# Router's last tile in halves and in another order, first up product behind one gathered chunk, state turns, bias columns and counts moved into experts 0 and 1

## What is computed

```python
logits = h.astype(F32) @ w_router.astype(F32) + b_router.astype(F32)
top_val, top_idx = lax.top_k(logits, TOP_K)          # 4 of 32
gates = jax.nn.softmax(top_val, axis=-1)
...
gu = xblk.astype(F32) @ w_gate_up[e].astype(F32) + b_gate_up[e].astype(F32)
gate, up = gu[:, :D_FF], gu[:, D_FF:]
gate = jnp.minimum(gate, SWIGLU_LIMIT)
up = jnp.clip(up, -SWIGLU_LIMIT, SWIGLU_LIMIT)
glu = gate * jax.nn.sigmoid(SWIGLU_ALPHA * gate)
return ((up + 1.0) * glu) @ w_down[e].astype(F32) + b_down[e].astype(F32)
```

## Time and profile before

| what | us |
|---|---|
| three runs | 1222.46, 1224.19, 1226.62 |
| median | 1224.19 |
| the profiled execution's own time | 1225.74 |
| its span (first to last instruction) | 1223.7 |
| TensorE busy | 1194.6 |
| VectorE busy | 456.5 |
| ScalarE busy | 259.2 |
| last load issued | 1175.5 |

### The profile page before, as it was taken

How to read it: one execution, slowest core, us unless ns; L and a number is a source line. 1 busy time by engine, 2 the same in 40 slices (tenths; PEclk the granted TensorE clock), 3 DMA queues, 4 the chain that set the end, 5 groups by cost and what they waited for, 6 DMA issues and landing times.

```text
span 1223.7 us, 18270 instructions
## 1 busy us (share of the span) xinstructions
PE 1194.6 (98%) x7828; PEld 576.3 (47%) x7828; DVE 456.5 (37%) x963; ACT 259.2 (21%) x633; POOL 45.7 (4%) x105
## 2 busy tenths in 40 slices
PE   8999999999999999999999999999999999999997
PEld 6776777745433444444443444444443434343332
DVE  3367777754322332333232232333331332222234
ACT  3114434522221211111120112111111111120113
POOL 8000110100000000000000000000000000000000
PEclk9999999999999999999999999999999999999999
DMA  9732202498999999999999999999999999999994
GB/s 286 178 104 70 79 3 73 143 397 324 418 429 428 426 427 428 427 432 423 432 430 428 431 432 431 427 431 429 434 432 428 430 429 431 433 431 428 428 422 160
DMA packets 46236, 436.11 MB, mean 356 GB/s; under 512 B 9269, under 2 KB 24696, under 8 KB 29386
## 3 DMA queue, kind: packets, MB, share of 16 engines
q1 hardware_dynamic: 44916, 431.35, 85.2%
q0 software_dynamic: 1152, 3.54, 0.9%
q10 hardware_dynamic: 86, 0.02, 0.0%
HBM read 430.01 MB, written 4.89 MB: 355 GB/s over the span
## 4 chain that ended last, share of the span: by engine, by line
PE 84%; DMA 14%; DVE 1%; ACT 0%; issue 0%; SPq 0%; DVEq 0%; ACTq 0%
PE bank L1555 30%; PE bank L1589 15%; DMA ring<-in_w_gate_up 11%; PE bank L865 10%; PE bank L1530 7%; PE bank L1619 4%; PE bank L1327 3%; PE bank L1580 2%; DMA ring<-in_w_down 2%; PE bank L1080 1%; PE bank L852 1%; PE bank L1610 1%; PE bank L894 1%; PE bank L1057 1%; DMA hx<-in_state_shift 0%; PE bank L1650 0%
## 5 line engine op out<-in xcount | busy, mean ns | idle before, releaser
L1555 PE MATMUL bank<-ring,mix 128*64 128x512 f32 x1504 | 343.9, 597 | 5.9 <-DMA ring<-in_w_gate_up 5.9
L1555 PEld LDWEIGHTS bank<-ring,mix 128*64 128x64 f32 x1504 | 101.5, 136 | 204.3 <-issue 198.0
L1589 PE MATMUL bank<-ring,mix 128*64 128x512 f32 x736 | 167.8, 597 | 2.1 <-DMA ring<-in_w_down 2.0
L2854 DVE TENSOR_TENSOR hTb<-bank,w2a 128x512 f32<-128x512 f32 x32 | 22.1, 692 | 371.0 <-PE bank L1580 371.0
L2121 ACT ACTIVATE mix<-bank,nf 128x256 f32<-128x256 f32 x64 | 26.9, 470 | 454.1 <-PE bank L1530 454.1
L865 PE MATMUL bank<-hTb,ring 128*128 128x328 f32 (+1 forms) x416 | 121.9, 443 | 0.8 <-DVE hTb L2323 0.4
L1555 PE MATMUL bank<-mix 128*64 128x512 f32 x496 | 111.4, 595 | 4.1 <-DMA mix<-in_w_gate_up 3.9
L2906 DVE TENSOR_TENSOR mix<-mix,bank 128x512 f32<-128x512 f32 x70 | 48.2, 689 | 160.0 <-PE bank L1619 160.0
L1589 PEld LDWEIGHTS bank<-ring,mix 128*64 128x64 f32 x736 | 49.9, 136 | 91.0 <-issue 87.6
L865 PEld LDWEIGHTS bank<-hTb,ring 128*128 128x128 f32 x416 | 76.4, 190 | 34.0 <-issue 2.2
L1555 PEld LDWEIGHTS bank<-mix 128*64 128x64 f32 x496 | 35.3, 137 | 73.9 <-issue 69.9
(11 more groups left out here) (442 smaller groups left out, 1145.7 us busy)
## 6 DMA issues: line engine op xcount, KB each, us to landing
ring<-in_w_gate_up SPq DMA_DIRECT2D x31, 4096.0 KB, 25.6
ring<-in_w_gate_up SPq DMA_DIRECT2D x32, 2048.0 KB, 16.3
ring<-in_w_down SPq DMA_DIRECT2D x16, 4096.0 KB, 28.1
mix<-in_w_gate_up SPq DMA_DIRECT2D x11, 4096.0 KB, 26.3
ring<-in_w_down SPq DMA_DIRECT2D x11, 2048.0 KB, 16.5
mix<-in_w_down SPq DMA_DIRECT2D x5, 4096.0 KB, 29.6
mix<-in_w_gate_up SPq DMA_DIRECT2D x9, 2048.0 KB, 15.0
ring<-in_w_in SPq DMA_DIRECT2D x14, 1024.0 KB, 5.6
```

Source lines behind the costliest of these rows:

```text
L1555: last_ = mm(b_[64 * half:64 * half + 64, :].rearrange("s (p q) -> s p q", q=4), toks, cols[:, half], start=(c == 0), stop=(c == KT - 1))
L1589: last_ = mm(b_[r:r + 64, :], lhs, w[:, o:o + NCOL], start=(j == 0 and q == 0), stop=(j == 1 and q == 3))
L2854: v.tensor_tensor(halves(gg), halves(banks[3][:, :]), bias(e, 0), ALU.add).then_inc(S("g1"), 1)
```

## The change

1. The last half tile of the router (tile 1, columns 512 to 1023) is added, turned and copied in two quarters (`turn_half`, `out_add(4)`), and the logits of that tile wait for the quarters at products 4 and 6, and not once at the start. The selection of tile 0 is made half before, half behind these steps. `fold(2)` goes ahead of the rank products, and the gathers of samples and tile 0 are spread anew around them.
2. Chunk 1 of the first gather is put into bank 2, so that chunks 0 and 1 are in separate banks. Chunk 0 is signalled, scaled and copied by itself; the first up product waits for it alone (`chunk_bias_ready` 1).
3. `gather_first(2)`, `counts`, `sample_states(0)`, `(1)` and `turn_bias` move behind up products of expert 0, `sample_states(2)` and `(3)` into expert 1. The unit `bias` goes; its turn raises `unit_filled` as the third one beyond the units (`BIAS`). ScalarE's and VectorE's parts follow, and ScalarE's exponentials for the gates stand between the second and third pair of chunks.
4. SyncE's load of the down bias moves from ahead of piece 7 to ahead of piece 10 and waits for `BIAS`.

```diff
-        STURN = [banks[1], banks[1], banks[6], banks[7]]
+        STURN = [banks[6], banks[7], banks[6], banks[7]]
+        BIAS = len(UNITS) + 3
...
-            sync.wait_ge(S("unit_filled"), U("bias", 1))
-            load(bdr, A["b_down"][0], "w00_bdr_in")
             sync.wait_ge(S("gathered"), 1)
             load_piece(7)
             for k in range(FIRST, len(PIECES)):
...
+                if k == FIRST + 1:
+                    sync.wait_ge(S("unit_filled"), BIAS)
+                    load(bdr, A["b_down"][0], "w00_bdr_in")
                 load_piece(k)
...
+            def turn_half(x):
+
+                pe.wait_ge(S("xo_ready"), 6 + x)
+                b_ = free("h2T", 4 + x)
+                for c_ in range(2):
+                    o_ = 512 + 256 * x + P * c_
+                    last_ = nc.tensor.transpose(b_[:, P * c_:P * c_ + P], h[:, 1, o_:o_ + P], ident[:, :])
+                filled(last_, "h2T")
...
+                    if n_ == 2 and c_ in (4, 6):
+                        pe.wait_ge(S("h2T_ready"), 3 + c_ // 2)
...
-            gather_samples(0, 6)
-            turn(4)
-            gather_samples(6, KT)
-            sample_states(0)
+            gather_samples(0, 2, 3, 4, 5)
+            turn_half(0)
+            turn_half(1)
             logits(2)
-            pe.wait_ge(S("sel_ready"), 2)
-            gather_rows(0, 1)
+            gather_samples(1, 6, 7)
+            fold(2)
             free("rank", 1)
             ranks_of_others(2)
-            fold(2)
-            gather_rows(1, KT)
+            pe.wait_ge(S("sel_ready"), 2)
+            gather_rows(0, 4)
             ranks(1)
-            sample_states(1)
-            turn_bias()
+            gather_rows(4, KT)
             pe.wait_ge(S("sel_ready"), 3)
             gather_first(0)
-            gather_first(2)
-            counts()
...
-                    if part == 0 and c % 2 == 0:
+                    if e + c == 0:
+                        pe.wait_ge(S("chunk_bias_ready"), 1)
+                    elif e == 0 and c == 1:
+                        pe.wait_ge(S("xg_ready"), 1)
+                    elif part == 0 and c % 2 == 0:
                         pe.wait_ge(S("xg_ready"), 4 * q + c // 2 + 1)
                     up(e, c)
-                    if e == 0 and c in (1, 3):
-                        gather_first(c + 3)
-                    if e == 0 and c in (4, 5):
-                        sample_states(c - 2)
+                    if e == 0 and c in (0, 1, 3):
+                        gather_first(c + 3 if c else 2)
+                    if e == 0 and c == 2:
+                        counts()
+                    if e == 0 and c > 5:
+                        sample_states(c - 6)
+                    if e == 0 and c == 7:
+                        turn_bias()
+                    if e == 1 and c in (2, 4):
+                        sample_states(1 + c // 2)
...
+            choose_exact(sel_0, TORD[1], 0, 2)
             out_add(4)
-            choose_exact(sel_0, TORD[1]).then_inc(S("sel_ready"), 1)
```

More of the change, by code:

```diff
@@ L232, in psum_units @@
     end("xo", 4)
-    add("h2T", 1, (2,))
+    add("h2T", 2, (2, 1))
     add("logit", 1, (3,))
@@ L1654, in first_chunk, with gather_samples @@
             def first_chunk(c):
[L1656 to L1660, removed]
+                return banks[2][:, 0:256] if c == 1 else banks[4 + c // 2][:, 256 * (c % 2):256 * (c % 2) + 256]
+            def gather_samples(*chunks):
+                for c_ in chunks:
+                    mm(first_chunk(c_), rows_s[:, 256 * (c_ // 2) + c_ % 2:256 * (c_ // 2) + 256:2], sel_s[:, :], start=(c_ % 2 == 0 or c_ == 1),
                        stop=False, skip_group_check=True)
@@ L1672, in turn_bias @@
                 pe.wait_ge(S("nm_brow_in"), 32)
-                b_ = free("bias", 0)
                 for q_ in range(8):
-                    last_ = nc.tensor.transpose(b_[:, 64 * q_:64 * q_ + 64], brows[:, q_:DM:8], ident[64:P, 64:P])
+                    last_ = nc.tensor.transpose(banks[2][:, 64 * q_:64 * q_ + 64], brows[:, q_:DM:8], ident[64:P, 64:P])
                 filled(last_, "bias")
@@ L1699, in _ @@
             pe.wait_ge(S("h2T_ready"), 4)
-            gather_samples(0, 6)
-            turn(4)
-            gather_samples(6, KT)
-            sample_states(0)
+            gather_samples(0, 2, 3, 4, 5)
+            turn_half(0)
+            turn_half(1)
             logits(2)
-            pe.wait_ge(S("sel_ready"), 2)
-            gather_rows(0, 1)
+            gather_samples(1, 6, 7)
+            fold(2)
             free("rank", 1)
             ranks_of_others(2)
-            fold(2)
-            gather_rows(1, KT)
+            pe.wait_ge(S("sel_ready"), 2)
+            gather_rows(0, 4)
             ranks(1)
-            sample_states(1)
-            turn_bias()
+            gather_rows(4, KT)
             pe.wait_ge(S("sel_ready"), 3)
             gather_first(0)
-            gather_first(2)
-            counts()
-            for s, k in (("logit", 3), ("fold", 3), ("rank", 2), ("sout", 2), ("yc", 3), ("var", 3)):
+            for s, k in (("logit", 3), ("fold", 3), ("rank", 2), ("yc", 3), ("var", 3)):
                 pe.wait_ge(S(f"{s}_ready"), k)
@@ L2115, in tokens_out @@
             def tokens_out(n):
-                act.wait_ge(S("gathered"), n + 1)
                 b = banks[4 + n if n < 4 else 5]
                 for x in range(2):
+                    if n + x == 0:
+                        act.wait_ge(S("chunk_sout_turned"), 1)
+                    else:
+                        act.wait_ge(S("gathered"), n + 1)
                     c = 2 * (n % 4) + x
-                    ins = a(xg[n // 4 % 2][:, 256 * c:256 * c + 256], b[:, 256 * x:256 * x + 256], ACT.Copy,
+                    b_ = banks[2][:, 0:256] if n == 0 and x else b[:, 256 * x:256 * x + 256]
+                    ins = a(xg[n // 4 % 2][:, 256 * c:256 * c + 256], b_, ACT.Copy,
                             scale=nf2[int(n // 4 >= EW // 4)][:, c:c + 1])
+                    if n + x == 0:
+                        ins.then_inc(S("chunk_bias_ready"), 1)
                 ins.then_inc(S("xg_ready"), 1)
             def sample_states(q):
-                act.wait_ge(S("sout_turned"), q + 1)
+                act.wait_ge(S("chunk_sout_turned"), q + 2)
                 ready(cp(sout[q].rearrange("p j k -> p (j k)"), STURN[q][:, :]), "sout")
@@ L2155, in _ @@
             row_norm(2)
[L2156 to L2160, removed]
+            tokens_out(0)
+            tokens_out(1)
             act.wait_ge(S("notm_ready"), 3)
@@ L2696, in out_add @@
                         signal(v.tensor_tensor(o, o, b[64 * w:64 * w + 64, :], ALU.add), "xo_ready")
-                else:
+                elif x < 4:
                     o = h[:, tile, 512 * w:512 * w + 512]
                     signal(v.tensor_tensor(o, o, b[:, :], ALU.add), "xo_ready")
+                else:
+                    for y in range(2):
+                        o = h[:, tile, 512 * w + 256 * y:512 * w + 256 * y + 256]
+                        signal(v.tensor_tensor(o, o, b[:, 256 * y:256 * y + 256], ALU.add), "xo_ready")
             def low_rows(n):
@@ L2741, in ranked, with choose_exact @@
                 signal(ins, "rank_ready")
-            def choose_exact(o, tile):
-                for x in range(4):
+            def choose_exact(o, tile, x0=0, x1=4):
+                for x in range(x0, x1):
                     last_ = v.tensor_scalar(o[:, CAP * x:CAP * x + CAP], iota[:, 0:CAP], rnk[:, tile, x:x + 1], None, ALU.is_equal)
@@ L2814, in _ @@
             choose_exact(sel_s, TORD[0]).then_inc(S("sel_ready"), 1)
+            choose_exact(sel_0, TORD[1], 0, 2)
             out_add(4)
-            choose_exact(sel_0, TORD[1]).then_inc(S("sel_ready"), 1)
[L2817 to L2820, removed]
+            to = TOFF[1]
+            for x in range(2):
+                signal(v.tensor_copy(hT[:, 4 + 2 * x:6 + 2 * x, to:to + P],
+                                     wait_filled("h2T", 4 + x)[:, 0:256].rearrange("p (c t) -> p c t", t=P)), "h2T_ready")
+            choose_exact(sel_0, TORD[1], 2, 4).then_inc(S("sel_ready"), 1)
             signal(v.tensor_copy(lgT[2][:, :], wait_filled("logit", 2)[:, 0:P]), "logit_ready")
```

32 lines of the change are left out of this document (20 added, 12 removed).

## The result

| kernel | median us | runs | ratio of the runs to those before | 95% interval |
|---|---|---|---|---|
| before | 1225.14 | 6, 1222.46 to 1227.55 | | |
| changed | 1234.68 | 6, 1232.99 to 1235.85 | 1.007 | 1.0058 to 1.0082 |

The change makes the kernel slower: by 9.5 us between the medians, by 7.1 to 10.0 us after the interval of the ratio. The span of the profiled execution is 1233.4 us, 9.7 more than before.

A forecast was written before the change was run, and what follows sets the result against it. The load stream was taken as the bound. Idle queue after 284 us of 14.75 against 4.95 us gave 9.8 us, the landings 8 to 8.7; 9.3 was added to the median 1224.19, giving 1233.5 us, range 1229.0 to 1237.0.

The forecast's parts named there:

- What bounds the kernel: Whole span: the end is when the load stream has no more gaps, plus the bytes left over 428 GB/s.
- rival 1: TensorE sets the end and the load stream absorbs the 9 us; TensorE's 0.5 us are the gain, 1223.7; chance 0.06.
- The router's chain: Router's last half tile in quarters: fold 1.55 us earlier (1.0 to 1.9), piece 7 issued at 295.15, not 296.73.
- TensorE's own gain: Expert 0's end: 1.17 us of waiting at 316.89 covered, less some 0.6 us of new waits: 0.5 us gained.
- The wait on SyncE: Pieces 10 to 12 stand behind the bias turn, ending at 315.3; piece 10 goes out at 315.8, not 306.20.
- The size: Load stream after 284 us: 9.3 us later, between 6.5 and 11.5; chance of this forecast 0.72.
- 8 to 8.7: Second way, through the landings of pieces 10 and 12: loss of 8 to 8.7 us.
- the sum of 9.8: Idle load queue after 284 us: 4.95 us before, 14.75 after, so the stream is 9.8 us later.
- Where it comes out: Chain of waits: TensorE's first wait for weights moves from 867 us to 600 to 660 us.
- The sum of the waits: TensorE's waits for weights sum to some 21 us in place of 12.
- The figure of 358 GB/s: Loads ahead of the gap: 4.2 MB would last 11.7 us, the gap 1.9 us shorter, the whole 1231.6 us.
- Rival 2: New wait passed early: hole before piece 7 shrinks, end 1 to 1.5 us earlier, 1222.9; chance 0.05.

The follow-up runs named there:

- first experiment: The changed kernel with SyncE's load of the down bias and its wait moved behind pieces 10 to 13: 1225.64 us, ratio 1.0004 to the kernel before.
- the four kernels of the table with a gap: Half the gap (wait ahead of piece 11), the gap alone in the kernel before, changed, longer gap: 4.2, 7.2, 9.5 and 14.2 us slower than before.

## Why the prediction was right, step by step

Predicted were 1233.5 us (1229.0 to 1237.0) and slower by over 0.3%; measured are 1234.68 and a ratio whose interval lies wholly above 1.003. The mechanism of the loss was right; its size was right in part by luck.

- **What bounds the kernel.** The loads, and not the engine that is busy for 98%. Shown by the two runs with 3.9 us more of TensorE for nothing and one instruction on SyncE for 7.2 us. The prediction's rival 1 (the gap is absorbed) is out.
- **The router's chain.** The fold's result is used at 290.85, 1.1 us before the 291.94 of the earlier trace rows, and 1.55 us earlier when the 0.5 us of offset are taken off: 1.55 was the term. The choice starts at 293.30 (before 294.39). Piece 7 was put at 295.15 and went out at 295.50, the first up product at 295.2 and was at 295.80, both right within 0.15 us after the offset.
- **TensorE's own gain.** The 1.17 us of waiting at the turn of gate and up are gone, and new waits of 0.25, 0.33 and 0.17 us stand before. As foretold it doesn't show in the time.
- **The wait on SyncE.** The bias turn was put at 315.3 and ended at 316.2, 0.4 us late after the offset. Pieces 10 to 12 stood behind it, and the share in 308 to 316 was 0.00 and 0.21, about the 0.1 foretold.
- **The size.** 9.3 us were taken from two sums, of 9.8 and of 8 to 8.7; 9.5 were measured, 7.1 to 10.0 after the interval. The removal of that wait alone (first experiment) gives all of it back. But the sum of 9.8 has a slip: of the 1.5 us of hole ahead of piece 7, 1.55 us less and 0.8 us more make 0.75, not 2.3. Put right, the idle queue is 13.2 us and not 14.75, the stream 8.2 us later and not 9.8, and the forecast would have been about a microsecond lower. What hid it is that the hole did not shrink: 5.1 us idle from 284 to 300, before 4.7. No term of the prediction says why; that all four early state outputs, and not only 0.8 us of them, left this stretch is one part (4 x 128 KB, an estimated 1.2 us at 430 GB/s), and the rest is open.
- **Where it comes out.** The first wait was foretold for 600 to 660 us and is at 642. The sum of the waits was put at 21 us and the view shows 18.4 (8.8, 7.9 and 1.7), 6.6 more than before. With the 3.5 us by which the busy time grew, 1.4 of them at half clock, that makes up the longer span.
- **The figure of 358 GB/s** that the Trainium skill gives for a core's loads from HBM (DMA: Bandwidth & Descriptors, Where 436 GB/s comes from) would have made the loss 1.9 us smaller. The trace of after has 426 GB/s in 320 to 340 and 430 on average from 344 to 1180, so that the measurement decides against it in this case of one busy core.

One price beside the forecast was wrong. Rival 2 said that without the new wait the change would be 1 to 1.5 us faster. The first experiment is that case and gives no difference, 0.9995 to 1.0013. The rival was priced from piece 7 alone, without the state outputs that no longer fill the hole. The prediction's sum has more idle queue beside the gap than before (5.75 us against 4.95), but only by the slip above.

## What to carry to other kernels

In a kernel that streams its weights, look at the DMA windows before the engines' busy shares, and ask of each load that waits what is queued behind it and for how long the queue can do without. A small load with a late condition belongs behind the large ones whose condition comes earlier. A gap costs its full length, to within half a microsecond in the four kernels of the table with a gap; it is paid hundreds of us later, and TensorE shows no wait at its place. Loads brought forward, on the other hand, gained nothing that could be told here, as the slots behind them came free no earlier.

## What the runs showed beside that

The kernel is nearer to a balance of the two than the chain of waits suggests. TensorE's 11.8 us of waits look like room for 11.8 us of work. The 136 transposes spread over four experts cost 4.8 us, and put in one place 11.1 us. The lead in time was about 10 us at that point (an estimate: eight experts of 1.2 us until 867), but the lead is in loads already issued, and those were through the queue within 13 us of the last issue. And 2.2 us of loads brought forward at 300 us were lost again by 600 us, with the DMA share never below 0.95 in a window of 10 us: small shortfalls show in GB/s (383 against 431) sooner than in the share (0.98).
